# Two transformer blocks on one core: the opening of the second block with one closed-form root for two norms in a row, the context side made ready inside the last layer, and pooling one side at a time

## What is computed

```python
def rmsnorm(x, g):
    y = x * rsqrt(mean(x * x) + EPS); return y * g

# end of block 1, last layer
pg = sigmoid(rmsnorm(x, ple_norm) @ w_ple_gate)
x = x + pg * (p @ w_ple)
h_lat = rmsnorm(x, final_norm)                      # first norm
# opening of block 2, layer 0
a_l = rms_norm(h_lat, norm_g[0, 0]) * (1 + sc1) + sh1   # second norm
a_c = rms_norm(ctx,   norm_g[0, 0]) * (1 + csc1) + csh1
h_lat = h_lat + g1  * pool_mix(a_l, pool_w, pool_scale)
h_ctx = ctx   + cg1 * pool_mix(a_c, pool_w, pool_scale)
# then: norm, modulation and a squared-ReLU MLP on both sides, an
# attention layer, a second MLP, the final norm
```

## Time and profile before

| | |
|---|---|
| median of 3 runs | 1945.79 us (1943.06 to 1945.81) |
| profiled execution, its own time | 1947.21 us |
| span of that execution | 1945.4 us |
| PE busy | 1796.2 us, 92% of the span |
| POOL, ACT, DVE busy | 1131.7, 870.5, 828.1 us |
| TensorE clock granted, mean | 0.96 |

### The profile page before, as it was taken

One profiled execution on the slowest core, in us unless ns is written; L12 is line 12 of the kernel. 1 busy time (PEld: TensorE's weight loads), 2 busy tenths in 40 slices (PEclk: granted clock), 3 DMA queues, 4 the chain that ended last, 5 costly groups with the idle time before them and its releaser, 6 DMA issues.

```text
span 1945.4 us, 32357 instructions
## 1 busy us (share of the span) xinstructions
PE 1796.2 (92%) x13076; PEld 1628.3 (84%) x13076; DVE 828.1 (43%) x1911; ACT 870.5 (45%) x1353; POOL 1131.7 (58%) x611
## 2 busy tenths in 40 slices
PE   7888999999988989999999479999999898889997
PEld 6787899999987878999999457778777677679997
DVE  6677444313466774443234652121212355542223
ACT  5534546444654445464446643132313233354443
POOL 6656578887776665778887113433434233137884
PEclk9889999999998999999999789999999989989999
DMA  6453365555454534655555335343444533124552
GB/s 243 149 203 110 123 216 180 184 187 188 163 188 169 172 124 147 222 175 187 178 188 168 132 123 188 136 149 135 149 161 172 208 132 113 41 82 163 188 178 90
DMA packets 70165, 311.49 MB, mean 160 GB/s; under 512 B 7680, under 2 KB 9984, under 8 KB 69760
## 3 DMA queue, kind: packets, MB, share of 16 engines
q1 hardware_dynamic: 68400, 306.47, 45.8%
q10 hardware_dynamic: 1616, 2.95, 0.4%
HBM read 308.34 MB, written 1.05 MB: 159 GB/s over the span
## 4 chain that ended last, share of the span: by engine, by line
PE 75%; DVE 8%; ACT 5%; POOL 4%; DMA 3%; issue 2%; DVEq 1%; ACTq 0%; SPq 0%
PE bank L858 22%; PE bank L862 21%; PE bank L861 21%; POOL wlo L826 4%; DMA raw<-in_stream 3%; PE bank L873 2%; ACT whi L1255 2%; PE bank L881 1%; PE bank L1022 1%; PE bank L1052 1%; DVE acts L2153 1%; PE bank L1132 1%; PE bank L1036 1%; DVE split_acts L1654 0%; PE bank L1184 0%
## 5 line engine op out<-in xcount | busy, mean ns | idle before, releaser
L826 POOL TENSOR_TENSOR wlo<-raw,whi 128x320 fp32r<-128x320 f32 (+1 forms) x607 | 1131.5, 1888 | 792.7 <-ACT whi L1255 792.4
L858 PE MATMUL bank<-split_acts,whi 128*128 128x256 f32 (+1 forms) x3540 | 1086.6, 307 | 57.6 <-DVE split_acts L1654 37.8
L861 PE MATMUL bank<-split_acts,whi 128*128 128x256 f32 (+1 forms) x3540 | 1069.6, 302 | 0.0
L862 PE MATMUL bank<-split_acts,wlo 128*128 128x256 f32 (+1 forms) x3540 | 1069.2, 302 | 0.0
L858 PEld LDWEIGHTS bank<-split_acts,whi 128*128 128x128 f32 x3540 | 685.9, 194 | 115.6 <-issue 52.8
L862 PEld LDWEIGHTS bank<-split_acts,wlo 128*128 128x128 f32 x3540 | 687.1, 194 | 21.8
L861 PEld LDWEIGHTS bank<-split_acts,whi 128*128 128x128 f32 x3540 | 687.8, 194 | 20.5
L1255 ACT ACTIVATE whi<-raw 128x1280 fp32r<-128x1280 f32 x367 | 464.3, 1268 | 492.3 <-PE bank L858 259.2
L2202 DVE SCALAR_TENSOR_TENSOR acts<-bank,acts 128x256 f32<-128x256 f32 x120 | 54.3, 481 | 236.2 <-PE bank L862 230.8
L1654 DVE TENSOR_TENSOR split_acts<-bank,split_acts 128x256 fp32r<-128x256 f32 (+1 forms) x204 | 98.8, 484 | 64.7 <-ACT split_acts L1356 19.9
L2216 DVE TENSOR_SCALAR acts<-bank 128x512 f32<-128x512 f32 (+1 forms) x64 | 35.7, 558 | 212.1 <-PE bank L862 212.1
(11 more groups left out here) (245 smaller groups left out, 1549.1 us busy)
## 6 DMA issues: line engine op xcount, KB each, us to landing
raw<-in_stream SPq DMA_DIRECT2D x463, 640.0 KB, 3.9
acts<-in_x SPq DMA_DIRECT2D x1, 1024.0 KB, 6.4
acts<-in_ctx ACTq DMA_DIRECT2D x1, 1024.0 KB, 7.9
acts<-in_const ACTq DMA_DIRECT2D x1, 1024.0 KB, 5.1
out<-acts SPq DMA_DIRECT2D x8, 128.0 KB, 2.1
acts<-in_const SPq DMA_DIRECT2D x1, 708.0 KB, 8.8
acts<-in_p ACTq DMA_DIRECT2D x2, 256.0 KB, 4.0
acts<-in_const ACTq DMA_DIRECT2D x1, 320.0 KB, 3.1
```

Source lines behind the costliest of these rows:

```text
L826: last = nc.gpsimd.tensor_tensor(wlo[slot][:, cols], raw[source][:, cols], whi[slot][:, cols].bitcast(F32), ALU.subtract)
L858: first = nc.tensor.matmul(out_ap, w_hi, hi_act(k), start=(k == 0), stop=False)
L861: nc.tensor.matmul(out_ap, w_hi, lo_act(k), start=False, stop=False)
L862: last = nc.tensor.matmul(out_ap, w_lo, hi_act(k), start=False, stop=(k == k_tiles - 1))
```

## The change

- **One root instead of two.** With m the mean of x squared and m' that of (g x) squared, g the first gain, the two reciprocal roots of the two norms multiply to one: 1 / sqrt(m' + EPS m + EPS EPS). Both sums are made inside the last loop: ACT squares x with and without g, side by side (`opening_squares`), DVE adds 512 columns (`opening_sum`), and one instruction joins them. The gain g goes into the modulation's gain (`opening_gains`). The modulation reads x itself. The first norm's own output, which the residual needs, comes later from a second, separate root (`("ss","root")`).
- **The context side inside the last layer.** Its squares and their sum stand beside the first "dn" products; its sum over partitions goes with that of the ple norm, its root behind that norm's; its scaling, modulation and split (`scale_ctx`, `modulate_split`, `low_ctx`) are in the rounds of the last loop. What the last layer prepared there for a next layer is gone.
- **Pooling one side at a time.** Tiles py and pool are now (side, group). The context's four groups come first, with the ada tiles between them, then x's. The pooling weights (chunks 243 to 245) are read twice and stay in the ring for it; chunk 245 is split in round 6 of the last loop. A root of one unused number (L1621 of the new kernel) stands on ACT ahead of the opening's first row copy. `r_first` lies in PSUM bank 7 now.

The order of the tiles:

```diff
+OPENING = pool_tiles(0)
+OPENING.insert(1, ("ss", "first"))
+OPENING.insert(OPENING.index(("pool", 0, 1)) + 1, ("ss", "root"))
 TILES2 = (
-    [("ss", "first")]
-    + [("ss", 0, 0)] + POOL_TILES
+    OPENING + pool_tiles(1)
     + [("ss", 0, 1)] + mlp_tiles(0)
...
-    {("py", 0, 0): 2, ("ss", 0, 1): 2, ("w1", 0, 0, 0): 2, ("w1", 0, 0, 4): 2,
+    {("ss", "root"): 2, ("py", 1, 0): 2, ("w1", 0, 0, 0): 2, ("w1", 0, 0, 4): 2,
```

PE, at the sum of the ple norm:

```diff
+                        if j == "ple" and lay == DEPTH - 1:
+                            pe.wait_ge(csq_used, KT)
+                            last = nc.tensor.matmul(half(b), ones[:, 0:128], c_sum, start=True, stop=True)
```

ScalarE, in the last layer:

```diff
+                    if lay == DEPTH - 1 and t[:2] == ("dn", 0):
+                        ctx_square(t[2])
...
+                if lay == DEPTH - 1:
+                    act.wait_ge(ctx_var, 1)
+                    sc.activation(var2[:, 0:256], var2[:, 0:256], ACT.Sqrt).then_inc(ctx_sd, 1)
+                    at = CONST2["band"][0]
+                    act.dma_start(const2, const2_in[:, 0:at]).then_inc(late_in, 16)
+                    act.dma_start(band, const2_in[:, at:]).then_inc(band_in, 16)
...
+                    elif t[0] == "pp":
+                        opening_squares(k)
+                    elif t[0] == "pg":
+                        modulate_split(0, 0, (0,), k, home=c_mod[k % 2])
```

ScalarE, in the opening:

```diff
+            sc.activation(stat[:, 14:15], stat[:, 13:14], ACT.Sqrt)
+            split_for((SECOND, ("py", 0, 3)))
...
+            take_rows(0, 0)
+            root2(("ss", "first"))
+            take_rows(0, 1)
             for t in range(KT):
-                modulate_split(0, 0, (0, 1), t)
...
+                modulate_split(0, 0, (1,), t)
+                if t == 1:
+                    take_rows(0, 2)
+                if t == 3:
+                    root2(("ss", "root"))
+                    take_rows(0, 3)
             scaled_before += KT
+            for g in range(4):
+                take_rows(1, g)
```

VectorE, in the last loop of the last layer:

```diff
+                        if t[0] == "pp" and k:
+                            opening_sum(k - 1)
+                        of_tile(t)
+                        if t[0] == "pg":
+                            if k == 0:
+                                dve.wait_ge(ctx_sd, 1)
+                                v.reciprocal(rstd2[:, 0:256], var2[:, 0:256])
+                                v.drain()
+                            scale_ctx(k)
+                            if k:
+                                low_ctx(k - 1)
...
+                    v.scalar_tensor_tensor(out=x_sums[:, 0:256], in0=x_sums[:, 256:512], scalar=EPS,
+                                           in1=x_sums[:, 0:256], op0=ALU.mult, op1=ALU.add).then_inc(norm_used, 1)
```

VectorE, in the opening:

```diff
+            for t in range(KT + 1):
+                if t < KT:
+                    x_scaled(t)
+                if t:
+                    x_low(t - 1)
+                if t in (1, 3):
+                    pool_out(0, t // 2)
+                if t == 3:
+                    b = arrived2(("ss", "root"))
+                    v.tensor_scalar(var_first, b[:, 0:256], 1.0 / D, EPS, ALU.mult, ALU.add)\
+                        .then_inc(tiles_out, EVICTS2[("ss", "root")])
+                if t in (5, 7):
+                    pool_out(0, t // 2)
...
+            v.reciprocal(r_first, var_first)
+            v.drain()
+            for t in range(KT):
+                v.scalar_tensor_tensor(out=side(h, t, 1), in0=tile(x, t),
+                                       scalar=par2[:, PAR2["first_g"] + t:PAR2["first_g"] + t + 1],
+                                       in1=r_first, op0=ALU.mult, op1=ALU.mult)
+                if t == 1:
+                    take_before2(("py", 1, 0))
...
+            for g in range(4):
+                pool_out(1, g)
```

More of the change, by code:

```diff
@@ L183, in chunk_reach @@
 def chunk_reach(tiles, spans, order, at):
-    reach, needed, adas = {}, 0, 0
+    reach, needed, adas, read = {}, 0, 0, 0
     for t in tiles:
-        needed = max(needed, -(-spans.get(t, (0, 0))[1] // CHUNK_ATOMS))
+        end = -(-spans.get(t, (0, 0))[1] // CHUNK_ATOMS)
+        read = max(read, end)
+        if t[1][:2] != ("py", 0):
+            needed = max(needed, end)
         adas += ADA_CHUNKS * (t[1][0] == "ada")
-        r = min(at[t] + AHEAD, len(order) - 1)
+        last = at[t] if needed == read else order.index(("split", needed - 1))
+        r = min(last + AHEAD, len(order) - 1)
         while r + 1 < len(order):
@@ L243, with evictions @@
 TILE_NO2 = {t: i for i, t in enumerate(TILES2)}
+def evictions():
+    out, rows = {}, 0
+    for t in TILES2:
+        if t[0] == "py":
+            rows += 1
+        else:
+            out[t], rows = 1 + rows, 0
+    assert all(n == 1 for t, n in out.items() if t[0] in ("ada", "turn"))
+    return out
+EVICTS2 = evictions()
 def second_spans():
@@ L249, in second_spans @@
         n = ATOMS_OF2.get(t[0], 0)
-        if t[0] in ("v", "py") and t[-1]:
+        if t[0] == "v" and t[-1]:
             out[t] = out[t[:-1] + (0,)]
+            continue
+        if t[0] == "py" and t[1]:
+            out[t] = out[("py", 0, t[2])]
             continue
@@ L1123, in gemm2 @@
-                    return
+                            last = nc.tensor.matmul(o, pool_lo[:, at:at + P], w_hi, start=False, stop=(k == 1))
                 elif kind == "pool":
-                    g = t[1] // 2
-                    if t[1] == 0:
+                    c, g = t[1:]
+                    if (c, g) == (0, 0):
                         pe.wait_ge(band_in, 16)
-                    pe.wait_ge(rows_out, g + 1)
-                    for s in range(2):
+                    pe.wait_ge(rows_out, c * 4 + g + 1)
@@ L1130, in gemm2 @@
+                    for j in range(2):
                         for kb in range(2):
[L1131 to L1132 removed]
+                            at, first = c * 512 + kb * 256 + j * P, 112 * kb
+                            last = nc.tensor.matmul(b[:, j * 256 + first:(j + 1) * 256],
                                                     token_rows[g % 2][:, at:at + P],
@@ L1585, in _ @@
+            squares2(both_sides, lambda k: tile(h, k, 512), lambda k: moved_out2(("pool", 1, k // 2)))
             root2(("ss", 0, 1))
@@ L2243, in final_of_first @@
-            def final_of_first(tiles):
-                for t in tiles:
-                    v.scalar_tensor_tensor(out=side(h, t, 1), in0=tile(x, t),
-                                           scalar=par2[:, PAR2["first_g"] + t:PAR2["first_g"] + t + 1],
-                                           in1=r_first, op0=ALU.mult, op1=ALU.mult)
-            final_of_first(range(3))
-            mods = mod.rearrange("p (l k t s) -> p l k t s", l=DEPTH, k=6, s=2)
-            gains = gain.rearrange("p (l i t s) -> p l i t s", l=DEPTH, i=2, s=2)
@@ new lines, in _, with pool_out @@
+            v.drain()
+            def pool_out(c, g):
+                b = arrived2(("pool", c, g))
+                for j in range(2):
+                    n = 2 * g + j
+                    last = v.scalar_tensor_tensor(out=side(h, n, c), in0=b[:, j * 256:(j + 1) * 256],
+                                                  scalar=pool_gate[:, 2 * n + c:2 * n + c + 1], in1=side(h, n, c),
+                                                  op0=ALU.mult, op1=ALU.add)
+                last.then_inc(tiles_out, EVICTS2[("pool", c, g)])
```

296 lines of the change are left out of this document (160 added, 136 removed).

## The result

| | before | changed |
|---|---|---|
| median | 1947.0 us (7 runs, 1943.06 to 1948.92) | 1936.38 us (7 runs, 1933.12 to 1939.79) |
| span of the profiled execution | 1945.4 us | 1934.0 us |

The ratio is 0.9949 (95% interval 0.9936 to 0.9961). The change is faster by 10.6 us; 1926.9 with a range of 1922 to 1935 was forecast. The sign was right and the size was not: of the 18.9 us forecast, 10.6 came, and the median lies 1.4 above the range.

What follows compares the result with a forecast made beforehand. Bound: a chain of waits between the last loop and the first MLP product, nearly 87 us for some 23 of pooling work. That product 18.9 earlier: 1947.2 less 18.9 is 1928.3, against the median 1926.9 us; range 1922 to 1935.

Steps and rivals of the forecast that it cites:

- The last update of x, "0.8 later": End of the last loop: last update of x 0.8 us later, between 0.5 earlier and 2.2 later.
- some 3.1 us of work in a round: Last loop: VectorE's work per round, with one scaling more and a sum of 512 columns.
- the tail behind it shortens from 2.3 to 1.1: Last loop: time from TensorE's last product to the last update of x falls from 2.3 to 1.1 us.
- ends some 2.0 later: Last loop: TensorE ends some 2.0 us later because the first round is late, at 1075.4.
- TensorE sets the pace at 3.6: Last loop: TensorE's 30 passes at 0.12 us need 3.6 a round, more than ScalarE's ring or VectorE.
- The rival in which the loop becomes the bound: Last loop: added work joins the ring, rounds grow 1.2 to 1.4 us, kernel takes 1937.3; chance 0.10.
- The first tile of x 14.3 earlier: After the last update: ScalarE starts x's first tile at 1083.1 instead of 1097.39, 14.3 us earlier.
- Chunk 246: Between x's tiles on ScalarE: a wait of 1.5 us for this chunk, then 1.26 of work.
- The last ada tile "beside this and not behind it": Pooling: TensorE's last ada tile ends about 1097.6, beside VectorE's work for x's second group, ready at 1099.5.
- x's groups and the next norm: After the ada tiles: groups 16.3 us earlier at 1113.0; next norm saves 2.6 more, first MLP product 18.9 earlier.
- The clock: Pooling: rival in which TensorE's clock stays at 1.2 GHz, kernel takes 1951.6 us; chance 0.04.

Runs made afterwards that it cites:

- experiment 1: Changed kernel with the context's modulated tile in one PSUM bank, two banks for x's squares, and the low part before the next scaling: 1931.72 us, ratio to before 0.9921.
- experiment 7: Changed kernel with one ada tile moved to the front of block 2 and chunk 246 split right behind the first root: 1929.25 us, ratio to before 0.9903.
- experiment 3: Changed kernel with the modulated tile in one PSUM bank, the low part still behind the next scaling: 1934.51 us, ratio to before 0.9941.
- experiment 9: Changed kernel without the one-column root ahead of the variance: 1937.0 us, ratio to before 0.9945.
- experiment 8: Changed kernel with ScalarE's high part of chunk 246 behind all tiles of x: 1939.25 us, ratio to before 0.9962.

## Why the prediction was right in sign and wrong in size

- **The last update of x, "0.8 later"**: failed, it came 5.1 later by the mark. The forecast was 32.3 from the mark for the end of TensorE's last product and a tail of 1.1 behind it. The changed kernel has 34.6 and 3.1, experiment 1 has 33.6 and 2.0, experiment 7, where the clock did not fall, 32.1 and 2.3. So three terms failed. First, the count of "some 3.1 us of work in a round" for VectorE leaves no room for a wait: the low part, 0.42 before, got a second input in SBUF and once took 3.21. That is 2.1 of the 4.3 us missing (changed kernel less experiment 1). Second, "the tail behind it shortens from 2.3 to 1.1": without that wait it was still 2.0, 0.9 more. Third, the fall of the clock behind the first round's idle time, counted nowhere: 1.3 (33.6 against 32.3). Where the clock did not fall, "ends some 2.0 later" was right, and the last update was 1.8 later, inside the stated bounds; one execution shows this. The first term also needs the third: experiment 7 has the same operands and lost little by them.
- **TensorE sets the pace at 3.6**: right once the low part is short (3.60 in experiments 1 and 3). The rival in which the loop becomes the bound did not come true: its loop was to be 10.4 over the forecast and was 4.3, and modulation and sum did not join the ring. That its 1937.3 lies close to the measured 1936.38 is chance; the rest was lost elsewhere.
- **The first tile of x 14.3 earlier**: the way from the last update to it was forecast as some 7 and is 6.45. Right; the table load's 1.1 in it was not due to the added root (experiment 9) but to a load that does not wait for the variance.
- **Chunk 246**: a wait of 1.5 was forecast, it was 3.55. TensorE gave the buffer free some 10.5 us after the last update and not 9.2, and its next content took 4.1 to land, not 3.5.
- **The last ada tile "beside this and not behind it"**: failed. It ended at 1104.2, 24.0 after the last update, where 21.1 was forecast (1097.6 less 1076.5). Some 2.5 us of the difference are sizes: the buffer free 1.3 later, and two landings of 4.1 in place of 3.5. Experiments 7 and 8 show that it decides. The path that the prediction took for the bound, VectorE's work ahead of x's second group, takes over once the stream is out of the way: TensorE waits 1.08 us for it in experiment 7. Of the 2.9 us, 1.0 came back in x's groups; the other 1.9 are those missing behind A.
- **x's groups and the next norm**: from the last ada tile to the end of the last addition (1118.56) it took 14.4, where 15.4 was forecast. No turn tile stood between the eight sums and the sum over the partitions: TensorE started 0.14 after them. From the variance to the first eviction it took 20.3, as before.
- **The clock** in the opening was at 1.2 GHz (passes at 0.21) only from 1083 to 1087 and 1104.8 to 1106.5; that rival was rightly small there. The fall that cost 1.3 us lay in the last loop, where the prediction did not look.

Of the miss of 9.5 us, 6.2 are these two places and 1.2 is the median of the kernel before, now 1947.0 and not 1945.8. The remaining 2.1 lie outside the marks, where the program is the same and executions differ by more; what makes them differ was not tried, and a trace of one execution each can't tell it.

## What to carry to other kernels

Price a moved instruction by where its operands now lie: a VectorE instruction that gets a second SBUF input next to a busy GpSimd can take GpSimd's whole duration, and either a PSUM home or a place in the order that starts it near the end of GpSimd's instruction avoided it here. Where transfers are freed by the work they feed, follow the chain through the buffers as far as the first product that needs it, and put the tile that frees a buffer where TensorE is idle anyway. In a loop that keeps one engine full, a delay in its first round was not made good later; and compare such edits by marks in the trace, since here the rest of the same program took between 784.0 and 790.5 us.

## What the runs showed of the hardware

- VectorE with two SBUF inputs waited for GpSimd's 2.96 us instruction and ended 0.27 to 0.29 us after it, in every meeting in which GpSimd had begun first (3.21, 1.17, 0.54); from PSUM it took 0.42 in the same meeting.
- The table load ran ahead of the wait of the root that needs it (experiment 9), with no drain behind it.
- About the same idle time of TensorE, 2.04 to 2.25 us, was followed by a fall of the granted clock in ten profiles and not in an eleventh (0.83 and 1.00 over ten microseconds). What decides is open.
